# MLP down projections by one level of Strassen's scheme in a two-block transformer kernel

## The reference, cut to what matters

```python
def sq_relu_mlp(h, w_up, w_down):
    return jnp.square(jax.nn.relu(h @ w_up)) @ w_down        # 1024 -> 4096 -> 1024

for i in range(DEPTH_2):                                      # two layers
    ...
    f = sq_relu_mlp(rmsnorm_2(x, g[2]), w_mlp_up[i], w_mlp_down[i])
    x = x + rmsnorm_2(f, g[3])
    gate = jax.nn.sigmoid(rmsnorm_2(x, g[4]) @ w_ple_gate[i])
    e = (p[i] @ w_ple_proj[i]) * gate
    x = x + rmsnorm_2(e, g[5])
```

## Time and profile before

| | |
|---|---|
| median of three runs | 1752.91 us (1752.72 to 1754.52) |
| span of the profiled execution | 1752.1 us |
| PE busy, matmuls | 1734.0 us (99%), 8325 |
| PE weight loads busy | 1435.6 us (82%) |
| DVE busy | 1043.1 us (60%) |
| ACT busy | 744.1 us (42%) |
| POOL busy | 167.0 us (10%) |
| mean granted TensorE clock | 0.997 of full speed |

### The profile page before, as it was taken

The page is one execution under the profiler, slowest core; times in us unless marked ns, Lnnn a source line. Parts: engine busy times, 40 slices in busy tenths (PEclk is TensorE's granted clock), DMA queues, the critical chain, the costliest instruction groups (busy, mean ns, idle before and its releaser), DMA issues.

```text
span 1752.1 us, 21988 instructions
## 1 busy us (share of the span) xinstructions
PE 1734.0 (99%) x8325; PEld 1435.6 (82%) x8325; DVE 1043.1 (60%) x1438; ACT 744.1 (42%) x1102; POOL 167.0 (10%) x145
## 2 busy tenths in 40 slices
PE   9999999999999999999999999999999999999998
PEld 7988877888798897788888888868887888888877
DVE  6478866776567777573535354775567544444466
ACT  4266764665426666441212123642225222222345
POOL 2011212000300000210000001320003000000031
PEclk9999999999999999999999999999999999999999
DMA  8222123214232222223232323313332332223321
GB/s 272 80 66 72 43 71 96 73 49 144 73 107 75 73 73 79 72 97 98 95 100 92 103 92 106 98 61 116 98 102 72 103 97 96 96 96 96 108 73 48
DMA packets 165543, 160.36 MB, mean 92 GB/s; under 512 B 13929, under 2 KB 158854, under 8 KB 165206
## 3 DMA queue, kind: packets, MB, share of 16 engines
q1 hardware_dynamic: 165302, 159.19, 29.1%
q10 hardware_dynamic: 160, 0.07, 0.0%
HBM read 150.43 MB, written 4.19 MB: 88 GB/s over the span
## 4 chain that ended last, share of the span: by engine, by line
PE 95%; DVE 2%; ACT 2%; issue 0%; DVEq 0%; ACTq 0%
PE bank L828 29%; PE bank L830 29%; PE bank L829 29%; PE bank L1148 2%; PE bank L1172 1%; PE bank L1073 1%; PE bank L1062 1%; DVE act_a L2073 1%; ACT act_a L1485 1%; DVE work L2099 1%; PE bank L1388 0%; PE bank L986 0%; PE bank L971 0%; DVE bank L2094 0%; PE bank L1163 0%
## 5 line engine op out<-in xcount | busy, mean ns | idle before, releaser
L828 PE MATMUL bank<-act_a,split_weights 128*128 128x512 f32 (+1 forms) x1400 | 550.7, 393 | 5.3 <-DVE act_a L2071 2.0
L830 PE MATMUL bank<-act_a,split_weights 128*128 128x512 f32 (+1 forms) x1400 | 544.1, 389 | 0.0
L829 PE MATMUL bank<-act_a,split_weights 128*128 128x512 f32 (+1 forms) x1400 | 543.8, 388 | 0.0
L1430 ACT ACTIVATE split_weights<-raw_weights 128x2048 fp32r<-128x2048 f32 x110 | 209.9, 1908 | 328.7 <-PE bank L830 328.7
L828 PEld LDWEIGHTS bank<-act_a,split_weights 128*128 128x128 f32 x1400 | 262.4, 187 | 64.5 <-issue 5.8
L2013 DVE TENSOR_TENSOR split_weights<-raw_weights,split_weights 128x2048 fp32r<-128x2048 f32 x110 | 253.9, 2308 | 92.7 <-ACT split_weights L1430 89.3
L830 PEld LDWEIGHTS bank<-act_a,split_weights 128*128 128x128 f32 x1400 | 262.2, 187 | 55.8
L829 PEld LDWEIGHTS bank<-act_a,split_weights 128*128 128x128 f32 x1400 | 262.5, 188 | 51.2 <-issue 0.2
L828 PE MATMUL bank<-act_b,split_weights 128*128 128x512 f32 x664 | 259.2, 390 | 0.0
L829 PE MATMUL bank<-act_b,split_weights 128*128 128x512 f32 x664 | 258.3, 389 | 0.0
L830 PE MATMUL bank<-act_b,split_weights 128*128 128x512 f32 x664 | 258.3, 389 | 0.0
(11 more groups left out here) (239 smaller groups left out, 2049.6 us busy)
## 6 DMA issues: line engine op xcount, KB each, us to landing
raw_weights<-in_w_mlp_up SPq DMA_DIRECT2D x32, 1024.0 KB, 5.4
raw_weights<-in_w_mlp_down SPq DMA_DIRECT2D x32, 1024.0 KB, 5.2
raw_weights<-in_w_in SPq DMA_DIRECT2D x18, 1024.0 KB, 5.3
raw_weights<-in_w_conv_in SPq DMA_DIRECT2D x12, 1024.0 KB, 5.1
raw_weights<-in_w_attn_in SPq DMA_DIRECT2D x16, 512.0 KB, 4.8
raw_weights<-in_w_ple_gate SPq DMA_DIRECT2D x8, 1024.0 KB, 5.2
raw_weights<-in_w_out SPq DMA_DIRECT2D x4, 1024.0 KB, 5.1
raw_weights<-in_w_attn_in SPq DMA_DIRECT2D x4, 1024.0 KB, 5.2
```

What stands on the lines that cost most here:

```text
L828: nc.tensor.matmul(dst, w[0], a[0], start=first, stop=False)
L829: nc.tensor.matmul(dst, w[0], a[1], start=False, stop=False)
L830: mm = nc.tensor.matmul(dst, w[1], a[0], start=False, stop=last)
L1430: nc.scalar.activation(wsp[:, pl.slot, 0, :], raw[:, pl.slot, :], ACT.Copy)\
```

## The change

Each down unit becomes 4 k-tiles by 512 output features. In it every pair of k-tiles, pair of output tiles and the two halves of the tokens (256 each) form a 2 x 2 by 2 x 2 block product, computed with seven products in place of eight. A unit holds 2 x 2 such groups, so it is 7 x 4 calls of `three` with 256 columns, 84 matmuls (`mlp_down` on PE). The seven products p of a chunk and an output half o go into seven PSUM banks; two units (parts 0 and 1) accumulate into them, one after the other.

- **Weights.** Four of the seven weight operands are sums or differences; POOL makes them for each unit (`weight_sums`: s1 and s2 from L3204 and L3206, s3 L3207, s4 L3214) into one buffer `sums`, s1 once the unit has landed and the unit before has split its fourth product, s4 once that unit is wholly split. ACT and DVE split each product's 128 x 512 weights by themselves (`product_hi`, `product_lo`, step p), into a ring of eight places: product n waits until PE is done with product n - 8.
- **Hidden values.** ACT alone squares; DVE makes the four token-half sums (T, y) and the low parts of seven operands (b, t, v); a unit of hidden features is ready after step v. PE waits at the first product of the first down unit (D0) for the first two up units (U0, U1) of the chunk, at that of the second (D1) for all four.
- **Results.** DVE adds seven product banks per output half into seven accumulators (a). In the last chunk the accumulators are combined into the output: DVE `mix` (x) and `last_product` (l), POOL `mix_far` and `add_kept`, ACT `keep_first` (k).
- **Squares at the end.** POOL adds six squares, with three accumulator sums between; PE adds POOL's sum, then two matmuls of 256 columns on the last square and one on the one before.
- The orders of steps are tables (`ACT_MLP`, `DVE_MLP`); the loops over chunks are written out. `keep_array_busy` fills with matmuls of 256 columns in place of 512.

```diff
+        SUMMED = {1: 1, 2: 2, 3: 0, 6: 3}
+        PLAIN = {0: (0, 0), 4: (1, 1), 5: (0, 1)}
+        OPERAND = ("b11", "t2", "t3", "t1", "t4", "b21", "b22")
+        FREES_NEXT = (21, 23, 25, 27)
+        ACT_UP = "p0 p1 p2 p3 s2 b2 t2 v2 p4 p5 p6 p7 s3 b3 p8 t3 p9 v3 "
+        ACT_MLP = ("s0 b0 t0 v0 s1 U3 b1 t1 v1 " + ACT_UP + PRODUCT_STEPS + " n0 n1 n2 n3",
...
+                   "U2 s0 b0 t0 v0 U3 s1 b1 t1 v1 " + ACT_UP + "p10 p11 p12 p13 p14 p15 k0 p16 p17 p18 p19 j0 p20 p21 "
+                   "p22 q0 p23 q1 p24 q2 p25 q3 p26 p27 k1 n0 n1 q4 q5 q6 q7")
+        DVE_UP = "e2 p0 p1 p2 p3 T2 b2 y2 t2 v2 p4 p5 e3 p6 p7 T3 b3 y3 p8 t3 p9 v3 p10 p11 p12 p13 p14 "
+        DVE_DOWN = "p15 a0 p16 a1 p17 a2 p18 a3 p19 a4 p20 a5 p21 a6 p22 p23 p24 p25 p26 p27 a7 n0 a8 a9 n1 a10 n2 a11 a12 a13 n3"
...
+                   "e0 U2 T0 b0 y0 t0 v0 e1 U3 T1 b1 y1 t1 v1 " + DVE_UP + DVE_DOWN,
+                   "x0 x1 x2 x3 x4 x5 x6 e0 U2 T0 b0 y0 t0 v0 e1 U3 T1 b1 y1 t1 v1 " + DVE_UP +
+                   "p15 p16 l0 p17 l1 l2 p18 l3 l4 p19 l5 p20 l6 p21 l7 j0 p22 p23 p24 p25 p26 p27 "
+                   "l8 l9 l10 l11 l12 l13 l14 l15 h0 n0 n1")
...
+            def mlp_down(layer, name, c, d):
+
+                o, part = divmod(d, 2)
+                pl = Place(tab, name, 8 * c + 4 + d)
+                number = down_unit_number(layer, c, d)
+                pe.wait_ge(hid_ready, 4 * up_unit_number(layer, c, 2 if d == 0 else 4))
+                for i in range(PRODUCTS):
+                    if i < PRODUCTS - 1:
+                        pe.wait_ge(prod_split, (PRODUCTS - 1) * number + i + 1)
+                    else:
+                        pe.wait_ge(w_split, pl.u + 1)
+                    if part == 0 and o:
+                        pe.wait_ge(prod_read, products_read(layer, c, 0, i))
...
+                    for mp in range(2):
+                        for kp in range(2):
+                            at = (2 * kp + mp) * P
+                            pair = 2 * part + kp
+                            three(mlp_bank(name, i)[:, pair_cols(mp)], [w[hl][:, at:at + P] for hl in (0, 1)],
+                                  [hidden(OPERAND[i], hl, pair) for hl in (0, 1)], part == mp == kp == 0,
+                                  part == mp == kp == 1, prod_done if mp == kp == 1 else None)
...
+                def product_hi(c, at):
+                    d, i = divmod(at, PRODUCTS)
...
+                    if at < 8:
+                        act.wait_ge(tile_done, tab.end[tab.first[name] + 8 * c + 2 + at // 4])
+                    else:
+                        act.wait_ge(prod_done, products_done(layer, c, at - 8))
+                    nc.scalar.activation(by_blocks(product_weights(name, c, at, 0)), product_source(pl, i), ACT.Copy)\
+                        .then_inc(prod_hi if i < PRODUCTS - 1 else w_hi, 1)
...
+            def weight_sums(layer):
...
+                    if c == MLP_CHUNKS - 1:
+                        mix_far(layer)
+                    for d in range(4):
+                        if (c, d) == (MLP_CHUNKS - 1, 3):
+                            add_kept(layer, 0)
...
+                        pool.wait_ge(raw_landed[pl.slot], pl.landed)
+                        if number:
+                            pool.wait_ge(prod_split, (PRODUCTS - 1) * (number - 1) + 4)
+                        nc.gpsimd.tensor_tensor(s1, weight_part(pl, 1, 0), weight_part(pl, 1, 1), ALU.add).then_inc(sum_made, 1)
+                        pool.wait_ge(sum_made, 4 * number + 1)
+                        nc.gpsimd.tensor_tensor(s2, s1, weight_part(pl, 0, 0), ALU.subtract).then_inc(sum_made, 1)
+                        nc.gpsimd.tensor_tensor(s3, weight_part(pl, 0, 0), weight_part(pl, 1, 0), ALU.subtract)\
+                            .then_inc(sum_made, 1)
...
+                            pool.wait_ge(w_split, before.u + 1)
+                        pool.wait_ge(sum_made, 4 * number + 2)
+                        nc.gpsimd.tensor_tensor(s4, weight_part(pl, 0, 1), s2, ALU.subtract).then_inc(sum_made, 1)
...
+            def sum_mlp_squares(layer):
...
+                for k in range(2, KT - 2):
+                    if k == 4:
+                        add_kept(layer, 1)
+                    pool.wait_ge(sq_added, added + k)
+                    pool.wait_ge(sq_done, done + k + 1)
+                    nc.gpsimd.tensor_tensor(ssum[:, :], ssum[:, :], sq[:, (done + k) % 2, :], ALU.add).then_inc(sq_added, 1)
```

More of the change, by code:

```diff
@@ L1295, in mlp @@
             def mlp(layer):
-                chunks = D_FF // D
                 name = f"mlp{layer}"
-                base = n.add("in", KT) - KT
-                hid = n.add("hid", KT * chunks) - KT * chunks
-                def chunk(i, first=False, last=False):
-                    if first:
-                        first_units(name, base)
-                    for j in range(2 if first else 0, 8):
-                        pl = Place(tab, name, j, i, 8, chunks)
-                        if j < 4:
-                            unit(pl, KT, 256, 2, from_a)
-                        else:
-                            unit(pl, KT, 256, 2, from_b, (hid_ready, hid + KT * i) if j == 4 else None,
-                                 by_tile=last and j == 7)
@@ L1312, in mlp, with mlp_up @@
[L1312 to L1315 removed]
+                first_units(name, n.add("in", KT) - KT)
+                for c in range(MLP_CHUNKS):
+                    for u in range(2 if c == 0 else 0, 4):
+                        mlp_up(layer, name, c, u)
+                    for d in range(4):
+                        mlp_down(layer, name, c, d)
+            def mlp_up(layer, name, c, u):
+                pl = Place(tab, name, 8 * c + u)
+                pe.wait_ge(w_split, pl.u + 1)
+                tiles = [2 * u + m for m in range(2)]
+                dst = [mlp_bank(name, t) if c else bank(pl, m) for m, t in enumerate(tiles)]
+                for k in range(KT):
+                    for m, t in enumerate(tiles):
+                        if k == 0 and c == 0:
+                            empty(pl.tile, m)
+                        elif k == 0 and t < PRODUCTS:
+                            pe.wait_ge(prod_read, products_read(layer, c - 1, 1, t))
+                        elif k == 0:
+                            pe.wait_ge(tile_read, tab.tile[tab.first[name] + 8 * c])
+                        at = k * 256 + m * P
+                        three(dst[m][:, :], [weights(pl, hl, at, at + P) for hl in (0, 1)],
+                              [from_a(hl, k) for hl in (0, 1)], k == 0, k == KT - 1, tile_done if k == KT - 1 else None)
@@ L1863, in mlp, with hidden_square @@
-                chunk(0, first=True)
-                with act.Fori(1, chunks - 1) as i:
-                    chunk(i)
-                chunk(chunks - 1, last=True)
-                squared(KT, last=True)
+                f_squares[layer] = n["squares"]
+                def hidden_square(c, u):
+                    pl = Place(tab, name, 8 * c + u)
+                    for m in range(2):
+                        act.wait_ge(tile_read, pl.tile + m + 1)
+                        nc.scalar.activation(tmp[:, m, :], tmp[:, m, :], ACT.Square).then_inc(hid_square, 1)
@@ L2637, in mlp, with hidden_out @@
-                chunk(0, first=True)
-                with dve.Fori(1, chunks - 1) as i:
-                    chunk(i)
-                chunk(chunks - 1, last=True)
-                n.add("hid", KT * chunks)
+                def hidden_out(c, u):
+                    pl = Place(tab, name, 8 * c + u)
+                    for m in range(2):
+                        dve.wait_ge(tile_done, pl.tile + m + 1)
+                        src_ = mlp_bank(name, 2 * u + m) if c else banks[(pl.bank + m) % 4]
+                        V.scalar_tensor_tensor(out=tmp[:, m, :], in0=src_[:, :], scalar=0.0, in1=rstd[:, :], op0=ALU.max,
+                                               op1=ALU.mult).then_inc(tile_read, 1)
```

466 lines of the change are left out of this document (374 added, 92 removed).

## The result

The changed kernel takes **1761.47 us** (median of 4 runs, 1761.15 to 1762.29) against 1753.03 for the kernel before beside it (4 runs, 1752.72 to 1754.52): a ratio of 1.0046, 95% interval 1.0034 to 1.0058. It is slower by 8.4 us where 16 us less were forecast, and outside both ranges that the prediction names, 1731 to 1745 and 1725 to 1750. The profiled execution's span is 1759.9 us, 24.0 more than the 1735.9 of the forecast's sum.

What follows compares the result with a forecast made beforehand. PE's matmuls were taken to bound the MLP. Terms -26.2 + 4.0 + 3.6 + 2.4 = -16.2 us against 1752.1 give a 1735.9 us span; forecast 1736.7 us, own range 1731 to 1745, wider range 1725 to 1750.

Steps and rivals of the forecast that it cites:

- Matmuls: PE's down units: 84 matmuls of 256 columns at 119.8 ns replace 48 of 512; 32 units save 26.2 us.
- cheaper matmuls: Rival, 3%: fixed 13 ns hides behind the stream, 256 columns cost 113.3 ns, saving 43.5 us; total 1719 us.
- D1's first product: Start of D1 in all eight chunks: POOL's fourth sum delays v3, PE waits 0.5 us each, +4.0 us.
- D2's part: D2 in the last chunk: l7 comes 1.8 us late because of POOL's work, twice, +3.6 us.
- Hidden values of the first three up units: Hidden values before D0, with the next chunk's up-weight splits: over 5 us to spare, so no cost.
- The end: End of each MLP: q6 and q7 wait for POOL's adds, root starts 1.2 us later; two layers, +2.4 us.
- D1 waits longer: Rival, 9%: the ACT and DVE chain before D1 is 1 to 2 us longer, 8 to 16 us lost; 1745 to 1753.
- DVE becomes the bound: Rival, 10%: from D0's start to D3, POOL sums of 1.84 us hold DVE back, 37 us more; total 1773 us.
- its threshold of 1.56: POOL's time per weight sum, in us, from which DVE's losses decide against the change: 2.0 us a chunk.
- the prediction's own signs of being wrong: Product spacing over 125 ns, POOL sums of 1.6 us or more, PE waits on `split_weights`, or waits totalling over 15 us.
- No new waits: Rival, 20%: POOL's D0 sum falls into a DVE gap, last-chunk adds come earlier, only the end's 2.4 remains; 1729 us.

Runs made afterwards that it cites:

- the wait by operand: Changed kernel with D1's first product waiting only for its own operand and its second product for step v3: 1753.96 us, ratio 1.0002.
- with memsets: Changed kernel with POOL's four weight sums per unit replaced by one memset each of the same tiles, reading no SBUF: 1730.67 us, ratio 0.9870.
- memsets as long as real sums: Changed kernel with each weight sum replaced by three memsets in a row, some 1.7 us per sum, reading no SBUF: 1737.98 us, ratio 0.9912.
- Fillers in the wait: Changed kernel plus 9 filler matmuls ahead of D1's wait in a layer's first chunk and 12 ahead of the statistics' wait: 1752.93 us, ratio 0.9996.

## Why the prediction was wrong

**Matmuls: right.** 120.0 ns each (40.31 us / 336) against 119.8; 25.7 us saved against 26.2. The rival "cheaper matmuls" at 113.3 ns fell, and with it the Trainium skill's formula (page "TensorE: Matmul & The Clock Gate", section "Back-to-back issue gap"), which gives 109 ns for 256 columns at the full clock and which that section itself calls the spacing of an isolated matmul.

**D1's first product: right where it was worked out.** 0.5 us in each inner chunk, and v3 as its cause, are what the trace and the wait by operand show. The last chunks' 4.1 us against 4.6 come near, in part because two errors offset each other: D2's part is 1.3 us each against the 1.8 counted, D1's 0.5 and 0.9 against 0.5.

**"Hidden values of the first three up units ... have over 5 us. These cost nothing": wrong in the first chunk**, 11.9 us of the 24.0. The step took one chunk for all. In the first chunk units 0 and 1 end together, so DVE reaches the third unit some 5 us later against D0's start, and the three sums that meet b2 and y2 (3.3 us) have no slack to go into. The size of a single collision had been counted right (1.15 against 1.1); which of them have cover in which chunk had not. Without the collisions the late start costs nothing (40.31 us in the first chunk, too, with memsets).

**The end, "+2.4": wrong**, 12.9 us of the 24.0. The step said that l13 ends 1.9 us before the last product; it ended 2.2 us after it. It had followed POOL's last two squares, but not what stands ahead of them: `add_kept` and D3's sums on POOL, squares that wait for l7 ahead of ACT's splits, and six splits on DVE that meet POOL's adds and keep ready read-outs behind them. Per end, 1.2 forecast + 4.1 for l13 + 1.5 and 2.8 for the clock make 6.8 and 8.1 of the 7.0 and 8.3 measured. With single memsets the end took 8.57 us, 1.2 more than before. That is the forecast's own number, but by luck: it holds for sums that neither read SBUF nor take the 1.29 us that the forecast gave them, and with memsets as long as real sums the end took 12.77.

**The clock was missing from the sum**: 9.3 us, inside these two items. The earlier trace rows show 1.00, and no term asked what a wait of 4 us would do to it.

**The rivals.** "D1 waits longer" named the wait that grew, but for every chunk and by a longer chain of steps; it grew by 3.1 us in the first chunks alone, by the late start and the collisions. "DVE becomes the bound" had the right mechanism in the wrong place: three of the four sums took 1.6 to 1.7 us at the median,

```profile
L3204 POOL TENSOR_TENSOR sums<-raw_weights x32: 1285/1611/3415, 765.0 to 1663.6; 128x512 f32<-128x512 f32 x32
L3206 POOL TENSOR_TENSOR sums<-sums,raw_weights x32: 1276/1350/3221, 766.6 to 1665.4; 128x512 f32<-128x512 f32 x32
L3207 POOL TENSOR_TENSOR sums<-raw_weights x32: 1286/1736/1747, 767.9 to 1667.1; 128x512 f32<-128x512 f32 x32
L3214 POOL TENSOR_TENSOR sums<-raw_weights,sums x32: 1292/1714/3409, 769.1 to 1668.8; 128x512 f32<-128x512 f32 x32
```

above its threshold of 1.56, but not because the blocked pattern is dear (the minimum is 1.29, as for the plain add in the earlier trace rows): the rest goes with splits on DVE beside them. Inner chunks hid all of it but 0.5 us. So two of the prediction's own signs of being wrong came: sums of 1.6 us or more, and PE's waits, 20.7 us in total (10.0 + 9.1 + 1.6) where 15 was the limit. "No new waits", 1729, is nearly the run with memsets, 1730.7. The rule of the Trainium skill that the prediction weighed (page "SBUF — State Buffer", section "Who interferes with whom") agrees with the runs: two-input steps and sums that read SBUF exclude each other for a whole instruction, and memsets, which only write it, do not disturb (all down stretches at 40.31 us).

## What to carry to other kernels

- Moving elementwise work from DVE to POOL does not free DVE where both read SBUF: here 16 sums cost DVE 8.4 us a chunk on POOL and 8.7 on itself. Put POOL's part beside DVE's reads from PSUM, or leave it on DVE, where its place in the line can be chosen.
- A steady chunk's slack says nothing of the first and the last one. Work both out on their own, with the same step list, and follow the last transfer of results through every engine that it passes.
- A new wait of PE of a few us may cost more than its length: ask for the clock behind it. Fillers in the wait (8.5 us), or a wait of 0.3 us in its place, brought that part back; waits of 1.8 us did not.
